# Feed-forward values finished in a PSUM bank, and unread wide products before the delta rule's waits, in a two-layer hybrid block kernel

## The reference, cut to what matters

```python
# one layer of block 1
o = bidir_gated_deltanet(qd, kd, vd, beta, g)        # chunks; each needs the inverse of (I + A), lower triangular
...
h = rmsnorm(x, norm_ffn_g[l])
u = centred_depthwise_conv(h @ w_up[l], ffn_conv_w[l])   # width 3: taps at -1, 0, +1
u_gate, u_val = jnp.split(u, 2, axis=-1)                 # 2816 channels each
x = x + (jax.nn.silu(u_gate) * u_val) @ w_down[l]
```

## Time and profile before

| what | us |
|---|---|
| median of 3 runs | 3676.53 |
| lowest and highest | 3672.08 and 3680.85 |
| profiled execution | 3675.34 |
| its span, first to last instruction | 3673.5 |
| mean granted clock of TensorE | 0.982 of full |
| TensorE busy | 3561.1 (97%) |
| VectorE, ScalarE, GpSimd busy | 1668.2, 983.5, 1809.2 |

### The profile page before, as it was taken

How to read it: one execution, slowest core, us unless ns; L and a number is a source line. 1 busy time by engine, 2 the same in 40 slices (tenths; PEclk the granted TensorE clock), 3 DMA queues, 4 the chain that set the end, 5 groups by cost and what they waited for, 6 DMA issues and landing times.

```text
span 3673.5 us, 49636 instructions
## 1 busy us (share of the span) xinstructions
PE 3561.1 (97%) x18684; PEld 2853.0 (78%) x18684; DVE 1668.2 (45%) x2654; ACT 983.5 (27%) x1752; POOL 1809.2 (49%) x1056
## 2 busy tenths in 40 slices
PE   8999899999999989999999999999999999999999
PEld 6766677788777767787887787888887788888887
DVE  5255645737425574573731353345343124344342
ACT  3236532201223463220121233232011124232010
POOL 5532346656653233665655434536666422536654
PEclk9999899999999989999999999999999999999999
DMA  3220122223231102332332211213223423212232
GB/s 130 81 75 30 36 70 92 92 92 98 85 120 64 47 2 81 95 103 78 101 98 87 80 53 58 75 61 97 92 94 102 102 88 97 75 58 93 96 92 92
DMA packets 85162, 299.20 MB, mean 81 GB/s; under 512 B 8840, under 2 KB 11016, under 8 KB 84616
## 3 DMA queue, kind: packets, MB, share of 16 engines
q1 hardware_dynamic: 83184, 291.16, 24.5%
q10 hardware_dynamic: 1032, 2.62, 0.6%
q0 software_dynamic: 784, 3.15, 0.3%
HBM read 285.88 MB, written 11.01 MB: 81 GB/s over the span
## 4 chain that ended last, share of the span: by engine, by line
PE 80%; DVE 10%; ACT 4%; issue 3%; DMA 1%; POOL 0%; DVEq 0%; ACTq 0%; SPq 0%; POOLq 0%
PE PSUM L390 19%; PE PSUM L389 19%; PE PSUM L388 19%; PE PSUM L960 2%; PE PSUM L2015 2%; PE PSUM L961 1%; PE PSUM L962 1%; DVE PSUM L558 1%; DVE SLABS L1636 1%; DVE OUTER_PRODUCT L1633 1%; PE PSUM L2019 1%; DMA SLABS<-w_k 1%; PE PSUM L1015 1%; DVE ACT_HI L1903 1%; PE PSUM L1572 1%
## 5 line engine op out<-in xcount | busy, mean ns | idle before, releaser
L299 POOL TENSOR_TENSOR W_LOS<-SLABS,W_HI 128x1024 fp32r<-128x1024 f32 (+3 forms) x454 | 1136.6, 2503 | 37.9
L297 POOL TENSOR_SCALAR W_HI<-SLABS 128x1024 fp32r<-128x1024 f32 (+3 forms) x454 | 504.9, 1112 | 1279.3 <-DMA SLABS<-w_k 1268.6
L389 PE MATMUL PSUM<-H_LO,W_HI 128*128 128x512 f32 x2448 | 967.6, 395 | 0.0
L388 PE MATMUL PSUM<-H_HI,W_HI 128*128 128x512 f32 x2192 | 868.9, 396 | 7.9 <-POOL W_LOS L299 5.1
L390 PE MATMUL PSUM<-H_HI,W_LOS 128*128 128x512 f32 x2192 | 871.0, 397 | 0.0
L389 PEld LDWEIGHTS PSUM<-H_LO,W_HI 128*128 128x128 f32 x2448 | 460.4, 188 | 116.7 <-issue 2.2
L388 PEld LDWEIGHTS PSUM<-H_HI,W_HI 128*128 128x128 f32 x2192 | 412.5, 188 | 109.4 <-issue 5.5
L390 PEld LDWEIGHTS PSUM<-H_HI,W_LOS 128*128 128x128 f32 x2192 | 411.9, 188 | 96.4
L558 DVE TENSOR_TENSOR PSUM<-PSUM,FACTORS 128x512 f32<-128x512 f32 x282 | 195.3, 695 | 552.0 <-PE PSUM L390 488.0
L388 PE MATMUL PSUM<-ACT_HI,W_HI 128*128 128x512 f32 x928 | 369.4, 398 | 10.1 <-DVE ACT_LO L1905 8.4
L390 PE MATMUL PSUM<-ACT_HI,W_LOS 128*128 128x512 f32 x928 | 371.6, 400 | 0.0
(11 more groups left out here) (516 smaller groups left out, 4996.6 us busy)
## 6 DMA issues: line engine op xcount, KB each, us to landing
SLABS<-w_k SPq DMA_DIRECT2D x406, 512.0 KB, 3.5
SLABS<-w_k SPq DMA_DIRECT2D x32, 768.0 KB, 4.2
SLABS<-w_k SPq DMA_DIRECT2D x32, 640.0 KB, 3.9
X<-w_k SPq DMA_DIRECT2D x2, 2048.0 KB, 9.3
SLABS<-w_k SPq DMA_DIRECT2D x16, 256.0 KB, 2.9
ARENA<-gate_rows SPq DMA_DIRECT2D x8, 512.0 KB, 5.4
bias_rows<-SQ ACTq DMA_DIRECT2D x1, 2560.0 KB
X<-xT SPq DMA_DIRECT2D x4, 512.0 KB, 6.9
```

What stands on the lines that cost most here:

```text
L297: nc.gpsimd.tensor_scalar(hi, raw, 1.0, 0.0, MUL, ADD).then_inc(pool_step, 1)
L299: nc.gpsimd.tensor_tensor(lo, raw, hi.bitcast(F), SUB).then_inc(slab_split[s], 1)
L388: mm(out, w_hi, rhs[0](k), start=k == first, stop=False)
L389: mm(out, w_hi, rhs[1](k), start=False, stop=False)
```

## The change

Two edits. In the feed-forward part of block 1 the second tap of the value half writes to bank 6 or 7 (`VALUES`) instead of its SBUF buffer, one column that this tap doesn't cover is copied there, and the product with the gate, the cast and the difference read and write that bank. In block 2 the same instructions as before are issued, only written in one line. In the delta rule TensorE gets products of the identity with the activation block A(0), 128x512 in float32, whose results nobody reads: three into bank 0 ahead of the first decay product, and two into bank 2 behind the second 32x32 products of each two pairs, but for the first two of direction 1.

```diff
+            def keep_clock(bank, products):
+                for _ in range(products):
+                    mm(bank[:], C("ident"), A(0), start=True, stop=True)
...
+            keep_clock(BANK[0], 3)
             pe.wait_ge(*nth("rows", 1))
             decays(0, 0)
...
                         last.then_inc(dn["t32_psum"], 1)
+                    if (d, p) != (1, 0):
+                        keep_clock(BANK[2], 2)
                     for u, b, q in both:
                         pe.wait_ge(*diag_blocks(d, p))
                         pe.wait_ge(*nth("t32", u + 1))
...
+        VALUES = [BANK[6], BANK[7]]
...
-                                last = nc.vector.scalar_tensor_tensor(buf[:, lo:hi], BANK[b][:, lo + o:hi + o], G(conv, col),
+                                to = VALUES[s] if n and part else buf
+                                last = nc.vector.scalar_tensor_tensor(to[:, lo:hi], BANK[b][:, lo + o:hi + o], G(conv, col),
                                                                       buf[:, lo:hi], MUL, ADD)
...
+                                if n == 0 and part:
+                                    nc.vector.tensor_copy(VALUES[s][:, SEQ - 1:SEQ], buf[:, SEQ - 1:SEQ])
...
                         dve.wait_ge(silu_done, need(silu_done))
+                        value = VALUES[s] if both else UP[s]
                         if both:
                             dve.wait_ge(bank_free[v], need(bank_free[v]))
-                            nc.vector.tensor_tensor(UP[s][:], GT[s][:], UP[s][:], MUL).then_inc(dve_step, 1)
-                            dve.wait_ge(dve_step, need(dve_step))
-                        else:
-                            nc.vector.tensor_tensor(UP[s][:], GT[s][:], UP[s][:], MUL).then_inc(dve_step, 1)
-                            dve.wait_ge(dve_step, need(dve_step))
+                        nc.vector.tensor_tensor(value[:], GT[s][:], value[:], MUL).then_inc(dve_step, 1)
+                        dve.wait_ge(dve_step, need(dve_step))
                         hi, lo = blk(ACT_HI, i * 2 + s), blk(ACT_LO, i * 2 + s)
-                        nc.vector.tensor_copy(hi, UP[s][:]).then_inc(dve_step, 1)
+                        nc.vector.tensor_copy(hi, value[:]).then_inc(dve_step, 1)
                         dve.wait_ge(dve_step, need(dve_step))
-                        nc.vector.tensor_tensor(lo, UP[s][:], hi.bitcast(F), SUB).then_inc(act_ready, 1)
+                        nc.vector.tensor_tensor(lo, value[:], hi.bitcast(F), SUB).then_inc(act_ready, 1)
```

## The result

| what | before | after |
|---|---|---|
| median (5 executions each) | 3672.08 | 3651.48 |
| lowest and highest | 3668.36 and 3680.85 | 3650.41 and 3652.69 |
| profiled execution | 3675.34 | 3651.78 |
| its span, and TensorE's mean granted clock | 3673.5, 0.982 | 3650.0, 0.987 |

The ratio is 0.9938, with a 95% interval from 0.9925 to 0.9951: about 23 us faster (the two medians of the table differ by 20.6), where I forecast 16.5 (3676.53 to 3660; the five executions of before include the three shown ahead). The median of 3651.48 lies inside the range of 3650 to 3669, near its lower end, outside the forecast case's own range (3654 to 3667), and next to rival B's 3650. The two profiled executions differ by 23.56 us (their spans by 23.5), and I account for that difference.

The account below looks back on a forecast made before the run. TensorE, with 80% of the chain that ended last, was taken to bound the kernel. 3675.3 - 12.2 - 4.7 = 3658.4 us, 3659.6 against the median, stated as 3660; range 3650 to 3669.

Parts of the forecast that it names:

- forecast case: Whole kernel: the feed-forward stall goes and part of the clock is kept, 3654 to 3667 us, chance 0.60.
- rival B: Delta rule: products hold the clock wherever they stand, new idle time costs nothing; 26.3 us faster, 3650 us, chance 0.13.
- Term 1: Block 1's feed-forward: the down projection's stall and the low clock behind it go, 6.1 us a layer, 12.2 in both.
- term 2: Delta rule: unread products keep TensorE's clock up in part, 2.3 us a layer, 4.7 us faster in both.
- the first place: Ahead of the first decay product: three unread products keep the clock with chance 0.4, worth 4.2 us a layer.
- the last pair: Direction 1's last pair: two unread products keep the clock with chance 0.65, worth 2.85 us a layer.
- Direction 0: Both its pairs: TensorE wins 2.4 us in each, but VectorE sets the end, so worth about 0.
- the loss: Direction 1's unprotected pair: new idle time of 4.1 us drops the clock, 2.7 us lost a layer, chance 0.45.
- C: Delta rule: products do nothing or only move the low clock; 3664 us, up to 3669 with the loss, chance 0.19.
- D: Block 1's feed-forward: the PSUM copy is held up too and the stall stays in part; 3672 us, chance 0.05.
- E: Block 1's feed-forward: VectorE's PSUM work is dearer than the rows say, so slower; 3686 us at 4 us a block, chance 0.03.

Follow-up runs that it names:

- Experiment 1: Changed kernel without the unread products, so the feed-forward edit alone: 3666.74 us, ratio 0.9972 to the kernel before.
- experiment 10: Changed kernel, but the product with the gate writes to SBUF, where cast and difference read it; only the product reads the bank: 3654.22 us, ratio 0.9932.
- experiment 11: Changed kernel with block 2's feed-forward values in the PSUM bank too: 3651.5 us, ratio 0.993 to the kernel before.
- Experiment 3: Changed kernel with two unread products instead of three ahead of the first decay product and one instead of two at the pairs: 3657.49 us, ratio 0.9953.
- Experiment 6: Changed kernel without the three unread products ahead of the first decay product; the pairs keep theirs: 3662.62 us, ratio 0.9961.
- experiment 4: Changed kernel without direction 0's unread products; those ahead of the first decay product and at direction 1's last pair stay: 3655.76 us, ratio 0.9937.
- experiment 5: Changed kernel with only the three unread products ahead of the first decay product, none at the pairs: 3667.28 us, ratio 0.9967.
- experiment 7: Changed kernel with three more unread products in TensorE's idle time ahead of direction 1: 3649.61 us, ratio 0.9936.
- experiment 9: Changed kernel with three more unread products ahead of direction 1 and one at its first two pairs: 3656.44 us, ratio 0.9943.

## Why the prediction was too cautious

**Term 1 was right, in mechanism and size.** Forecast 6.1 us a layer, measured 6.0 in both, and 6.0 again in experiments 1 and 10. The PSUM copy took 0.692 us (I took 0.67), the one-column copy 0.16 (0.16), product and difference 0.697 and 0.692 (0.70). The last low part came 8.7 us before it was asked for; I had 8.9. Experiment 1's ratio (10.3 us) has 12.0 within its interval. The kept 0.75 us of the tap became 0.76. What I didn't see is that the cast and the difference needn't have moved (experiment 10). Against the edit I had set the Trainium skill, "VectorE: DVE Perf Modes", section "Why PSUM operands drop a tier". The trace agrees with it on the size, 0.69 against 0.43 us at best in SBUF. But the product, which in SBUF took up to 2.62 us, takes 0.70 with its operand in the bank, and experiment 11 made VectorE 48 us less busy with the "slow" operand.

**The failed step was in term 2: how much of the clock the products keep, 0.4 x 4.2 + 0.65 x 2.85 - 0.45 x 2.7 = 2.3 us a layer.** The runs showed 5.8 and 6.0. The prices were near (4.3 measured for 4.2, and 2.8 for 2.85); what was wrong was mainly the chances 0.4 and 0.65, for the first place and the last pair kept the clock in both layers. That makes 2.6 and 0.95 us a layer. Direction 0 adds 0.7 that I had at nothing, and the loss, which I had counted with 1.2, came with 2.1 and 1.8.

The chances rested on a price that was too low by half: "an fp32 product of 128x512 costs 3.70 / 8 = 0.46 us at most in a row, 0.44 from start to start". The row that I divided, L1476 with x8, is four calls, not eight: `early(j)` issues `for k in range(4)`, and each float32 product stands there as two rows. I could have read that from the code beside the row. From 0.44 followed the idle remnants of 2.5 and 1.9 us, and from these the chances. The true remnants are 1.2 and 0.8 us, both shorter than the 1.9 of the shortest fall that I had found.

The wrong price isn't all of it. Experiment 3 has nearly the remnants that I assumed, and its profiled execution kept the clock at the last pair twice and at the first place once, the second time for over half of the gain; its delta rules are 5.6 and 5.5 us shorter than before, against my 2.3. So the chances were too low for those remnants too, as far as one execution can show. A remnant alone doesn't tell whether the clock falls: it fell without any at 394.21.

**The first place**: 4.2 us forecast if kept, 4.3 measured in both layers. Experiment 6 gives 4.1 and 2.9 for it.

**Direction 0 was "worth about 0", and that was half right.** In the changed kernel it is 0.7 us a layer, since VectorE sets the end. But experiments 4 and 5 show that without these products the clock can stay at half from the first pair into direction 1 (6.7 us in layer 0 of experiment 4), in a kernel whose stages have all moved a few us, while layer 1 of experiment 4 is faster without them. The kernel before happened not to have that stretch (its clock came back at 410.9). I priced the two pairs by the low stretch that I saw, not by the one that could come. What they are worth on average is open: by the ratios of all executions experiment 4 is as fast as the changed kernel.

**The loss at direction 1's first pair came, in both layers**, with 3.1 and 3.2 us of new idle time instead of 4.1 (the unread products take twice as long, and those of the second pair ran at half clock from 394.21). It cost 2.1 and 1.8 us instead of 2.7: the turning was at half (3.54 us), the queries' products behind it were not (1.16). I gave it 0.45. That the idle time brings it is only half shown: filling it (experiment 7) moved the fall behind the next 32x32 products, and one wide product there as well (experiment 9) removed it.

**The rivals.** B was nearest in time, with the clock kept at every protected place, but wrong in that the new idle time did cost. Its 26.3 us were 23.8 in the edited stages: it left out the loss (3.9) and direction 0's gain (1.4). That its 3650 lies within 1.5 us of the median is in part luck, as two more executions brought the median of before down from 3676.53 to 3672.08. C and D are out: the products alone gave 12.5 us, and the bank took the wait away. E is out: no operation on the bank was above 0.76 us. (E's figure for 4 us a block comes to 3690 by its own working, 1.4 us over in each of 22 turns less 16.9, not to 3686; nothing rests on it.)

**What I had no term for** is the clock elsewhere. It sums to +0.3 us here, out of stages from -2.45 to +6.22 that nobody edited. Those stages have idle times like the ones above, and which of them ends with a lower clock changes from one run to the next: in kernels that are the same up to that place, the first decay product stands anywhere from 324.75 us (experiment 11) to 331.92 (experiment 5). Why a given one falls was not settled, and no run here tried to.

## What to carry to other kernels

Before a row's time is divided by its count, find the loop in the code that issued it and compare the counts: here a float32 product is two rows. When idle time is filled to keep TensorE's clock, price the kernel without the filling by the low stretch that it could have, not by the one that the trace happens to show, and look at what the time won makes idle next. Before a difference in total time is credited to an edit, measure the edited stage between the same two instructions: experiment 3 was 5.5 us slower in total and 0.7 in the stage it changed. Where an operation on SBUF values shows a wide spread, ends when GpSimd's operation does, and the next engine waits for its chain, giving that one operation a PSUM operand can be enough.

## What was not expected of the hardware

- A float32 product of 128x512 takes 0.87 us at full clock and stands in the trace as two rows, 592 ns each when read alone; the fast format's takes 0.233 us from start to start. 18 products make L1448 x36.
- Once at half, the clock stayed there for most of 38 us with TensorE busy for 33.6 of them (0.51, experiment 4), in work that was mostly 32x32, 64x64 and 128x128 products.
- The granted clock fell behind 32x32 products with only 0.4 to 0.7 us of idle between them (experiment 7), and didn't where one 128x512 product, 1.1 us, followed them (experiment 9). It also fell behind 64x64 and 32x32 products with no idle time at all (394.21 in the changed kernel), and the same work kept it in one run and lost it in another (382.73 there, 386.71 in experiment 6).
- With the product out of SBUF, part of the delay moved to the next operations in SBUF: in experiment 10 the cast's median for one buffer was 802 ns against 427 before, its least value still 426.
